# Query blocks taken together in the first block's attention

## The chip, the cores and the metric

One core of a Trainium2 chip runs one program. The metric is the device time of one execution in microseconds, the median of the timed runs. The core has five engines that each run their own instruction list in order and meet at semaphores: TensorE (PE, with weight loads shown as PEld), VectorE (DVE), ScalarE (ACT), GpSimd (POOL) and SyncE (SP), which issues most DMAs.

## The reference

Two blocks of two layers each on one sequence of 512 positions, width 1024. The change touches only the attention of the first block. Each of its layers has three kinds of attention:

```python
oa = diff_attention(...)              # 4 heads, each the difference of two softmax maps; bias, causal
ob = mla_attention(...)               # 8 heads; scores = nope part + rope part; causal
oc = sliding_window_attention(...)    # 8 heads; window of 128 keys, sinks, bias
y = (gates[:, :, 0] * ((oa * silu(a_z)) @ w_br_a[l])
     + gates[:, :, 1] * ((ob * silu(b_z)) @ w_br_b[l])
     + gates[:, :, 2] * ((oc * silu(c_z)) @ w_br_c[l]))
x = x + rms_norm(y @ w_out[l], norm_post[l])
x = x + sigmoid(x @ w_ple_gate[l]) * (p[l] @ w_ple_proj[l])
```

In all three the query block i of 128 positions sees key blocks up to i: i+1 blocks in the first two, at most two blocks in the third. Retention, a dilated attention and two gated feed-forwards make the second block.

## The kernel before

All projections multiply weights split into a high and a low float32r part with an activation split the same way: three matmuls of 128x128 by 128x512 for each k-tile (method `kt`, lines L714 to L716), eight k-tiles for most output tiles. Weights stream in chunks of eight k-tiles through a ring of three slots; ACT makes the high part (L1250), POOL the low (L565, L567).

The attention of a layer is twelve items, n = 0 to 11: four of kind da (differential), four mla, four sw (sliding window). An item is a pair of maps or heads, m = 0 and 1, one on rows 0 to 63 of the array and one on rows 64 to 127. Its queries come in four blocks i. The steps for one block are

- scores on PE (`scores`, L852, for mla also L858 for the rope part) into banks 3 and 4, one for each m;
- maxima on DVE (`maxima`, L1882, L1887 or L1885): the bias or mask is added and the row's maximum taken, the scores go to SBUF (`probs`, two buffers for each m, block i uses number i % 2);
- the exponential with its sum on ACT (`exps`, L1388);
- probabilities on DVE (`probs`, L1900, L1904 or L1906 and L1909): divided by the sum; in da the two maps are joined;
- transposes on PE (`turn`, L879) into bank 5, for mla and sw also bank 6;
- a copy to SBUF on ACT (`copies_out`, L1398);
- values on PE (`values`, L899) into bank 7.

Around and between these lie the projections that later steps need. `ORDER[n]` lists the projection tiles beside item n, `STEPS[n]` their k-tiles, and `cuts(n)` gives the nine places at which the list is broken off. In items 0 to 6 the places are even: PE fills up to the first, gives the scores of block 1, fills, turns block 0, fills, gives scores of block 2 and values of block 0, and so on. From item 7 on (`ONE_PLACE`) two neighbouring places are one. Every engine follows the same list by `cuts`: what DVE evicts (`beside`, L1973 and others) and ACT converts stands between the attention steps in the same order.

Projection tiles, and the small column sums (`sum_da`, `sum_q`, `sum_kv`, L768) and row spreads (`row_*`, L777) among them, open the banks 0 to 2 in turn (`rotate(3)`). PE waits on the semaphore `evicted` when it opens a bank whose last tile DVE has not taken. In item 2 the list begins bkv, sum_da, sum_q, v; in item 3 kr, sum_kv, sum_da, cv. DVE's output of the item before (`out`, L1913, L1920) lies between `maxima(n, 0)` and `probs(n, 0)`, and for da items waits for ACT's square (L1415).

```python
for n in range(12):
    at_ = cuts(n)
    for i in range(QT):
        fill(n, at_[2 * i])
        if i + 1 < QT:
            scores(n, i + 1)
        if i:
            values(n, i - 1)
        fill(n, at_[2 * i + 1])
        turn(n, i)
```

Of the kernel before, what the change touches and what calls it, by code (L numbers as in the profile page):

```python
# [20 lines left out]
ALU = mybir.AluOpType  # L21
ACT = mybir.ActivationFunctionType

P = 128
# [77 lines left out]

def cuts(n):
# [203 lines left out]
def two_stacks_kernel(nc, d, out):  # L307
# [3 lines left out]
    with ExitStack() as ctx:  # L311
# [343 lines left out]
        def _(pe):  # L655
            t = Tally(pe)

            class Programs:
# [121 lines left out]
                def mix(self, l):  # L780
# [58 lines left out]
                    def scores(n, i):  # L839
                        kind = KINDS[n]  # L840
                        kb, blocks = key_blocks(kind, i)
                        keys = CK if kind == "sw" else AK
                        if i == 0:
                            pe.wait_ge(sems["evicted"], self.scored_on + 1)
                        t.up("scored", 2)
                        if self.steps:
                            pe.wait_ge(sems["scored"], t.at("scored"))
                        self.steps += 1
                        q, kk = slice(i * P, (i + 1) * P), slice(kb * P, (kb + blocks) * P)
                        for m in range(2):  # L850
                            r = slice(64 * m, 64 * m + 64)
                            ins = pe.matmul(banks[S0 + m][:, 0:blocks * P], AQ[r, q], keys[r, kk], start=True, stop=(kind != "mla"))  # L852
                            if kind != "mla":
                                ins.then_inc(sems["s_ready"], t.one("s_ready"))
                        if kind == "mla":
# [13 lines left out]
                    def turn(n, i):  # L869
                        _, blocks = key_blocks(KINDS[n], i)  # L870
                        if t.k.get("pt_copied", 0):
                            pe.wait_ge(sems["pt_copied"], t.at("pt_copied", CREDITS["pt_copied"]))
                        if i == 0:
                            pe.wait_ge(sems["v_token"], t.at("v_token"))
                        for m in range(group(KINDS[n])):
                            t.up("probs")
                            pe.wait_ge(sems["probs"], t.at("probs"))
                            for b in range(blocks):
                                ins = pe.transpose(banks[TURN + m][:, b * P:(b + 1) * P], SS[i % 2][m][:, b * P:(b + 1) * P], ID[:])  # L879
# [3 lines left out]
                    def values(n, i):  # L883
                        kind = KINDS[n]
                        kb, blocks = key_blocks(kind, i)
                        if i == 0:
# [4 lines left out]
                        for b in range(blocks):  # L891
                            for m in range(group(kind)):
                                r = slice(64 * m, 64 * m + 64)
                                if kind == "da":
                                    r, p = slice(0, P), PT[i % 2]
                                    v = VT[:, kb + b, :]
                                else:
                                    v, p = (CV if kind == "sw" else VT)[:, kb + b, r], PT[m]
                                ins = pe.matmul(banks[OUTB][r, i * P:(i + 1) * P], v, p[:, b * P:(b + 1) * P],  # L899
                                                start=(b == 0), stop=(b == blocks - 1))  # L900
# [16 lines left out]
                    for n in range(12):  # L917
                        at_ = cuts(n)
# [8 lines left out]
                        fill(n, at_[8])  # L927
# [1630 lines left out]
```

## Time and profile before

| | |
|---|---|
| Median of 3 runs | 2990.86 us (2988.71 to 2991.18) |
| Profiled execution, its own time | 2991.07 us |
| Its span | 2989.2 us |
| PE, PEld busy | 2949.5 us (99%), 2360.9 us (79%) |
| DVE, ACT, POOL busy | 1740.0 us (58%), 1055.6 us (35%), 1280.3 us (43%) |
| Attention of the first block with its projections | about 35 to 560 us and 600 to 1130 us |

The span is from the first to the last instruction; the execution's own time is 1.9 us longer. Durations in a timeline are from start to end, and matmuls overlap, so the time that one takes from the stream is read from one start to the next. A matmul of float32 operands appears as two in the counts. Item numbers and layers are read off the order of the lines.

### The profile page before, as it was taken

The numbers are of one execution on the slowest core, as the hardware profiler recorded it, in microseconds if no ns is written. First come the engines' busy times: TensorE is split into PE (matmuls) and PEld (weight loads), VectorE is DVE, ScalarE is ACT, GpSimd is POOL, SyncE is SP. The second block draws the span as 40 slices with busy tenths as digits, with TensorE's granted clock in tenths as the row PEclk, the third lists the DMA queues.
The fourth block names the chain that finished last, engine by engine and source line by source line (L and its number), as shares of the span: only waits on it lengthen the run. The fifth ranks groups of instructions, "written<-read, shape, count | busy, mean of one in ns | idle before, by whom it ended". The sixth has DMA issues, their size and how long they took to land.

```text
span 2989.2 us, 39167 instructions
## 1 busy us (share of the span) xinstructions
PE 2949.5 (99%) x15272; PEld 2360.9 (79%) x15272; DVE 1740.0 (58%) x3028; ACT 1055.6 (35%) x1875; POOL 1280.3 (43%) x926
## 2 busy tenths in 40 slices
PE   8999999999999999999999999999999999999999
PEld 6777777887777778788888788887888888788887
DVE  4765455475745555646553587615766666587722
ACT  4443343354343432533333322224333333432222
POOL 3333334453333345444444455544434334355543
PEclk9999999999999999999999999999999999999999
DMA  5222223232222223232222233332222222223332
GB/s 194 81 78 65 71 78 98 85 110 73 78 64 71 77 86 96 87 99 85 85 82 84 82 99 99 95 95 90 84 78 71 78 78 78 71 85 99 99 94 76
DMA packets 78332, 260.22 MB, mean 87 GB/s; under 512 B 10731, under 2 KB 13547, under 8 KB 78149
## 3 DMA queue, kind: packets, MB, share of 16 engines
q1 hardware_dynamic: 77572, 255.63, 27.6%
q8 instruction: 122, 2.00, 0.3%
q10 hardware_dynamic: 576, 2.10, 0.2%
q14 instruction: 62, 0.50, 0.1%
HBM read 255.53 MB, written 6.09 MB: 88 GB/s over the span
## 4 chain that ended last, share of the span: by engine, by line
PE 93%; DVE 3%; ACT 1%; DMA 1%; issue 1%; POOL 0%; SPq 0%; DVEq 0%; ACTq 0%
PE bank L714 25%; PE bank L716 25%; PE bank L715 24%; PE bank L852 2%; PE bank L899 2%; PE bank L879 1%; PE bank L731 1%; PE bank L732 1%; PE bank L738 1%; PE bank L1016 1%; PE bank L1017 1%; PE bank L1022 1%; PE bank L1111 1%; PE bank L768 1%; DMA bias_copies<-bias_vectors 1%
## 5 line engine op out<-in xcount | busy, mean ns | idle before, releaser
L565 POOL TENSOR_TENSOR w_lo<-w_raw,w_hi 128x512 fp32r<-128x512 f32 x458 | 609.8, 1332 | 1627.5 <-ACT w_hi L1250 1627.5
L714 PE MATMUL bank<-h_hi,w_hi 128*128 128x512 f32 x2367 | 944.7, 399 | 0.8 <-POOL w_lo L565 0.8
L716 PE MATMUL bank<-h_hi,w_lo 128*128 128x512 f32 x2367 | 924.6, 391 | 0.0
L715 PE MATMUL bank<-h_lo,w_hi 128*128 128x512 f32 x2367 | 923.3, 390 | 0.0
L1250 ACT CAST w_hi<-w_raw 128x1024 fp32r<-128x1024 f32 x458 | 480.1, 1050 | 1234.9 <-PE bank L716 1138.1
L567 POOL TENSOR_TENSOR w_lo<-w_raw,w_hi 128x512 fp32r<-128x512 f32 x458 | 667.3, 1457 | 35.9
L714 PEld LDWEIGHTS bank<-h_hi,w_hi 128*128 128x128 f32 x2367 | 445.4, 188 | 97.9 <-issue 9.3
L716 PEld LDWEIGHTS bank<-h_hi,w_lo 128*128 128x128 f32 x2367 | 445.1, 188 | 96.0
L715 PEld LDWEIGHTS bank<-h_lo,w_hi 128*128 128x128 f32 x2367 | 445.9, 188 | 86.4 <-issue 0.3
L2128 DVE TENSOR_SCALAR m<-bank,gains 128x512 f32<-128x512 f32 x48 | 36.1, 751 | 328.6 <-ACT ta L1453 197.0
L1388 ACT ACTIVATE probs<-probs,small_columns 128x128 f32<-128x128 f32 (+2 forms) x192 | 101.9, 531 | 168.6 <-DVE small_columns L1887 164.4
L716 PE MATMUL bank<-f_hi,w_lo 128*128 128x512 f32 x352 | 136.9, 389 | 0.0
L714 PE MATMUL bank<-f_hi,w_hi 128*128 128x512 f32 x352 | 136.9, 389 | 0.0
L715 PE MATMUL bank<-f_lo,w_hi 128*128 128x512 f32 x352 | 136.9, 389 | 0.0
L1882 DVE CUSTOM_DVE_ANT_0 probs<-bank,bias 128x256 f32<-128x256 f32 (+3 forms) x128 | 56.4, 441 | 93.8 <-PE bank L852 90.1
L1398 ACT COPY pt<-bank 128x256 f32<-128x256 f32 (+3 forms) x160 | 55.5, 387 | 62.3 <-PE bank L879 62.2
L714 PE MATMUL bank<-zo_hi,w_hi 128*128 128x512 f32 x192 | 77.3, 403 | 0.0
L715 PEld LDWEIGHTS bank<-f_lo,w_hi 128*128 128x128 f32 x352 | 66.1, 188 | 13.8
L716 PEld LDWEIGHTS bank<-f_hi,w_lo 128*128 128x128 f32 x352 | 66.1, 188 | 13.8
L714 PEld LDWEIGHTS bank<-f_hi,w_hi 128*128 128x128 f32 x352 | 66.1, 188 | 13.5
L731 PE MATMUL bank<-h_hi,w_hi 128*128 128x512 f32 x161 | 68.3, 424 | 8.2 <-ACT h_hi L1316 4.9
L716 PE MATMUL bank<-zo_hi,w_lo 128*128 128x512 f32 x192 | 75.0, 391 | 0.0
(321 smaller groups left out, 4473.2 us busy)
## 6 DMA issues: line engine op xcount, KB each, us to landing
w_raw<-in_w SPq DMA_DIRECT2D x458, 512.0 KB, 3.5
bias_copies<-bias_vectors SPq DMA_DIRECT2D x1, 2560.0 KB
x_res<-in_x_t ACTq DMA_DIRECT2D x4, 512.0 KB, 8.1
bias<-bias_copies SPq DMA_DIRECT2D x8, 256.0 KB, 3.3
bias<-bias_copies SPq DMA_DIRECT2D x16, 128.0 KB, 2.4
out_x<-x_res SPq DMA_DIRECT2D x8, 256.0 KB, 2.5
bias_copies<-bias_vectors SPq DMA_DIRECT2D x1, 1280.0 KB
ple_raw<-in_p_t SPq DMA_DIRECT2D x2, 512.0 KB, 3.7
```

Of the source, the lines that this page charges most:

```text
L565: pool.tensor_tensor(WL[slot][:, 0:half], RAW[slot][:, 0:half], WH[slot][:, 0:half].bitcast(F32), ALU.subtract).then_inc(sems["lo_half"], 1)
L567: pool.tensor_tensor(WL[slot][:, half:], RAW[slot][:, half:], WH[slot][:, half:].bitcast(F32), ALU.subtract).then_inc(sems["lo_done"], 1)
L714: pe.matmul(banks[bank][:], WH[slot][:, w], hi[:, k, :], start=start, stop=False)
L715: pe.matmul(banks[bank][:], WH[slot][:, w], lo[:, k, :], start=False, stop=False)
L716: pe.matmul(banks[bank][:], WL[slot][:, w], hi[:, k, :], start=False, stop=stop).then_inc(sems["kt_done"], 1)
L731: pe.matmul(banks[bank][:], WH[slot][:, w], hi[:, k, :], start=start, stop=False)
L852: ins = pe.matmul(banks[S0 + m][:, 0:blocks * P], AQ[r, q], keys[r, kk], start=True, stop=(kind != "mla"))
L899: ins = pe.matmul(banks[OUTB][r, i * P:(i + 1) * P], v, p[:, b * P:(b + 1) * P], start=(b == 0), stop=(b == blocks - 1))
L1250: act.copy(WH[slot][:], RAW[slot][:]).then_inc(sems["hi_done"], t.one("hi_done"))
L1388: act.activation(s, s, ACT.Exp, bias=sm(NM + u), accum_out=sm(DEN + u)).then_inc(sems["exped"], t.one("exped"))
L1398: act.copy(p[:, 0:w], banks[TURN + m][:, 0:w]).then_inc(sems["pt_copied"], t.one("pt_copied"))
L1882: dve.tensor_tensor_reduce(SS[i % 2][m][:, 0:w], banks[S0 + m][:, 0:w], bias, 1.0, LOWEST, ALU.add, ALU.max, sm(MX + u)).then_inc(sems["dv ...
```

## The change

Query blocks whose scores fit one bank of 512 columns are taken together as one part: blocks 0 and 1 (128 + 256 columns) in da and mla, then 2 and 3 alone; blocks 0 and 1 and blocks 2 and 3 (256 + 256) in sw. The steps run once for each part. Inside a part the blocks lie side by side (`placed_blocks`), each with its own matmuls, maximum, exponential, reciprocal and scaling as before; the transposes of a part end in one semaphore step, and ACT copies the part's whole width at once. The buffers alternate by a count of parts over all items (`parity`). `cuts` makes 2 x parts + 1 places. The number of tiles and k-tiles and their order are the same.

```diff
+TOGETHER = {"da": ((0, 1), (2,), (3,)), "mla": ((0, 1), (2,), (3,)), "sw": ((0, 1), (2, 3))}
+def n_parts(n):
+    return len(TOGETHER[KINDS[n]])
+def parity(n, part):
+    return (sum(n_parts(x) for x in range(n)) + part) % 2
+def placed_blocks(kind, part):
+    at_, placed = 0, []
+    for i in TOGETHER[kind][part]:
+        w = key_blocks(kind, i)[1] * P
+        placed.append((i, at_, w))
+        at_ += w
+    assert at_ <= SEQ
+    return placed
 def cuts(n):
-    total = sum(k for _, k in ORDER[n])
+    total, parts = sum(k for _, k in ORDER[n]), n_parts(n)
     if n >= ONE_PLACE:
...
-        places = [upto(n, round(third / 3 * (p + 1))) for p in range(3)] + [upto(n, total - BEHIND)]
+        early = max(parts - 1, 2)
+        places = [upto(n, round(third / early * (p + 1))) for p in range(parts - 1)] + [upto(n, total - BEHIND)]
         return [x for place in places for x in (place, place)] + [len(STEPS[n])]
     first = PRE if n == 0 else 0
-    share = (total - first) / 9
-    return [upto(n, round(first + share * (p + 1))) for p in range(9)]
+    share = (total - first) / (2 * parts + 1)
+    return [upto(n, round(first + share * (p + 1))) for p in range(2 * parts + 1)]
...
-                    def scores(n, i):
+                    def scores(n, part):
...
+                        placed = placed_blocks(kind, part)
+                        t.up("scored", 2 * len(placed))
+                        for i, at_, w in placed:
+                            kb = key_blocks(kind, i)[0]
+                            q, kk = slice(i * P, (i + 1) * P), slice(kb * P, kb * P + w)
                             for m in range(2):
                                 r = slice(64 * m, 64 * m + 64)
-                                pe.matmul(banks[S0 + m][:, 0:blocks * P], AR[r, q], KR[r, kk], start=False, stop=True).then_inc(sems["s_ready"], t.one("s_ready"))
+                                ins = pe.matmul(banks[S0 + m][:, at_:at_ + w], AQ[r, q], keys[r, kk], start=True, stop=(kind != "mla"))
+                                if kind != "mla" and i == placed[-1][0]:
+                                    ins.then_inc(sems["s_ready"], t.one("s_ready"))
...
-                        for i in range(QT):
+                        for i in range(parts):
                             fill(n, at_[2 * i])
-                            if i + 1 < QT:
+                            if i + 1 < parts:
                                 scores(n, i + 1)
...
                         for m in range(2):
+                            for i, at_, w in placed_blocks(kind, part):
+                                u = 2 * i + m
...
+                                dve.tensor_tensor_reduce(SS[parity(n, part)][m][:, at_:at_ + w], banks[S0 + m][:, at_:at_ + w], bias, 1.0, LOWEST, ALU.add, ALU.max, sm(MX + u)).then_inc(sems["dve_step"], t.one("dve_step"))
```

On PE, in a sw item, this stood before where block 2's scores, block 0's values and block 1's transposes are given (probs_71 and probs_72 hold block 1's probabilities of m = 0 and 1):

```order
L716 MATMUL bank<-h_hi,w_lo 128x512
L852 MATMUL bank<-c_k,att_q 128x256 x2
L899 MATMUL bank<-pt_73,c_v 64x128
L899 MATMUL bank<-pt_74,c_v 64x128
L879 MATMUL bank<-ident,probs_71 128x128 x2
L879 MATMUL bank<-ident,probs_72 128x128 x2
L714 MATMUL bank<-h_hi,w_hi 128x512
```

and this stands in the same item now, where the scores of blocks 2 and 3 and the transposes of blocks 0 and 1 are given:

```order
L746 MATMUL bank<-h_hi,w_lo 128x512
L884 MATMUL bank<-c_k,att_q 128x256 x4
L912 MATMUL bank<-ident,probs_69 128x128 x3
L912 MATMUL bank<-ident,probs_70 128x128 x3
L744 MATMUL bank<-h_hi,w_hi 128x512
```

Two pairs of score matmuls now follow each other, and all transposes of two blocks; the sw item is broken off at three places in place of five, the last scores and values at its end counted.

On DVE, at the head of item 2 (the 128 and 256 columns are blocks 0 and 1; rstd in L1920 is the output of item 1, lat_q the tile bkv), before:

```order
L1887 TENSOR_SCALAR small_columns<-small_columns 128x1
L1913 SCALAR_TENSOR_TENSOR ta<-ta,tc 128x512
L1920 SCALAR_TENSOR_TENSOR rstd<-bank,ta 128x512
L1900 RECIPROCAL small_columns<-small_columns 128x1 x2
L1906 TENSOR_SCALAR probs_70<-probs_70,small_columns 128x128
L1909 SCALAR_TENSOR_TENSOR probs_69<-probs_69,small_columns,probs_70 128x128
L1882 ISA probs_71,small_columns<-bank,bias 128x256
```

and now:

```order
L1921 TENSOR_SCALAR small_columns<-small_columns 128x1
L1947 SCALAR_TENSOR_TENSOR ta<-ta,tc 128x512
L1954 SCALAR_TENSOR_TENSOR rstd<-bank,ta 128x512
L1934 RECIPROCAL small_columns<-small_columns 128x1 x3
L1940 TENSOR_SCALAR probs_70<-probs_70,small_columns 128x128
L1943 SCALAR_TENSOR_TENSOR probs_69<-probs_69,small_columns,probs_70 128x128
L1934 RECIPROCAL small_columns<-small_columns 128x1
L1940 TENSOR_SCALAR probs_70<-probs_70,small_columns 128x256
L1943 SCALAR_TENSOR_TENSOR probs_69<-probs_69,small_columns,probs_70 128x256
L1916 ISA probs_71,small_columns<-bank,bias 128x384
```

The eviction of bkv (lat_q) comes behind the next two maxima in both; ahead of it now stand two more maxima, one more pair of reciprocals, two more scalings, and maxima of 384 columns in place of 256. In item 3 the same stands ahead of kr.

## Rows read from the trace of the kernel before

**Rows 1.** The page, part 4: shares of the last chain by engine.
```profile
PE 93%; DVE 3%; ACT 1%; DMA 1%; issue 1%; POOL 0%; SPq 0%; DVEq 0%; ACTq 0%
```

**Rows 2.** Waits of PE: line, releaser, total us, times, longest us.
```profile
PE bank L777 <- DVE att_q L1987: 1.5, 2, 0.9
...
PE bank L879 <- DVE probs L1909: 0.9, 1, 0.9
```

**Rows 3.** Timeline of PE, item 8, layer 0: start, duration, line, operands.
```profile
346.44 0.39 PE L714 MATMUL bank<-h_hi,w_hi 128*128 128x512 f32 x1
...
347.12 0.39 PE L714 MATMUL bank<-h_hi,w_hi 128*128 128x512 f32 x1
...
347.89 0.70 PE L852 MATMUL bank<-c_k,att_q 64*128 64x256 f32 x4
348.53 0.44 PE L879 MATMUL bank<-ident,probs 128*128 128x128 f32 x2
348.72 0.48 PE L714 MATMUL bank<-h_hi,w_hi 128*128 128x512 f32 x1
...
349.50 0.40 PE L714 MATMUL bank<-h_hi,w_hi 128*128 128x512 f32 x1
```

**Rows 4.** Timeline of PE, mla items, layer 0: a long and a short part.
```profile
247.08 1.02 PE L858 MATMUL bank<-k_rope,att_qr 64*128 64x512 f32 x4
248.04 0.66 PE L899 MATMUL bank<-pt,att_vt 128*64 128x128 f32 x8
248.63 0.50 PE L714 MATMUL bank<-h_hi,w_hi 128*128 128x512 f32 x1
...
263.39 0.39 PE L858 MATMUL bank<-k_rope,att_qr 64*128 64x128 f32 x4
263.71 1.09 PE L899 MATMUL bank<-pt,att_vt 128*64 128x128 f32 x16
264.74 0.66 PE L865 MATMUL bank<-ident,var 128*128 128x128 f32 x4
```

**Rows 5.** Timeline of PE, item 2, layer 0: from its first scores.
```profile
107.81 0.49 PE L852 MATMUL bank<-att_k,att_q 64*128 64x128 f32 x4
...
109.58 0.47 PE L714 MATMUL bank<-h_hi,w_hi 128*128 128x512 f32 x1
...
116.00 0.95 PE L768 MATMUL bank<-ones,da_sq 128*128 128x1 f32 x8
116.81 1.93 PE L768 MATMUL bank<-ones,lat_sq 128*128 128x1 f32 x16
118.60 0.63 PE L714 MATMUL bank<-h_hi,w_hi 128*128 128x512 f32 x1
```

**Rows 6.** Timeline of DVE, item 2, layer 0.
```profile
108.52 0.28 DVE L1882 CUSTOM_DVE_ANT_0 probs<-bank,bias 128x128 f32<-128x128 f32 x1
...
109.58 1.35 DVE L1913 SCALAR_TENSOR_TENSOR ta<-ta,tc 128x512 f32<-128x512 f32 x1
111.38 0.69 DVE L1920 SCALAR_TENSOR_TENSOR rstd<-bank,ta 128x512 f32<-128x512 f32 x1 [0.45 <-ACT da_sq L1415]
...
113.41 0.43 DVE L1882 CUSTOM_DVE_ANT_0 probs<-bank,bias 128x256 f32<-128x256 f32 x1 [0.17 <-PE bank L852]
...
114.07 0.42 DVE L1882 CUSTOM_DVE_ANT_0 probs<-bank,bias 128x256 f32<-128x256 f32 x1
...
116.20 0.69 DVE L1973 TENSOR_TENSOR lat_q<-bank,rstd 128x512 f32<-128x512 f32 x1 [1.51 <-PE bank L716]
```

**Rows 7.** DVE groups by shape, 35 to 1100 us: count, busy us, mean ns.
```profile
L1909 DVE SCALAR_TENSOR_TENSOR probs<-probs,small_columns,probs 128x256 f32<-128x256 f32 x8 | 8.7, 1088 | 0.3
...
L1906 DVE TENSOR_SCALAR probs<-probs,small_columns 128x256 f32<-128x256 f32 x8 | 6.5, 815 | 0.3
...
L1906 DVE TENSOR_SCALAR probs<-probs,small_columns 128x384 f32<-128x384 f32 x8 | 3.8, 479 | 0.3
```

**Rows 8.** Windows: us, busy by engine (instructions), granted clock, DMA share, GB/s.
```profile
118.60:122.44 3.84, 3.84 (x12) 2.94 (x12) 1.88 (x6) 2.86 (x6) 1.32 (x2) 0.56 0.32 93
```

More of the change, by code:

```diff
@@ L848, in scores @@
                         self.steps += 1
[L849 to L854, printed above, removed]
@@ L867, in turn_values, with turn, values @@
                         t.up("v_token")
-                    def turn(n, i):
-                        _, blocks = key_blocks(KINDS[n], i)
+                    def turn(n, part):
                         if t.k.get("pt_copied", 0):
                             pe.wait_ge(sems["pt_copied"], t.at("pt_copied", CREDITS["pt_copied"]))
-                        if i == 0:
+                        if part == 0:
                             pe.wait_ge(sems["v_token"], t.at("v_token"))
                         for m in range(group(KINDS[n])):
-                            t.up("probs")
+                            t.up("probs", len(TOGETHER[KINDS[n]][part]))
                             pe.wait_ge(sems["probs"], t.at("probs"))
-                            for b in range(blocks):
-                                ins = pe.transpose(banks[TURN + m][:, b * P:(b + 1) * P], SS[i % 2][m][:, b * P:(b + 1) * P], ID[:])
+                            for b in range(part_width(KINDS[n], part) // P):
+                                ins = pe.transpose(banks[TURN + m][:, b * P:(b + 1) * P], SS[parity(n, part)][m][:, b * P:(b + 1) * P], ID[:])
                             ins.then_inc(sems["turned"], t.one("turned"))
                             t.up("pt_copied")
-                    def values(n, i):
+                    def values(n, part):
                         kind = KINDS[n]
-                        kb, blocks = key_blocks(kind, i)
-                        if i == 0:
+                        if part == 0:
                             t.up("o_used")
@@ L890, in values @@
                         pe.wait_ge(sems["pt_copied"], t.at("pt_copied", CREDITS["pt_copied"]))
[L891 to L900, printed above, removed]
+                        for i, at_, w in placed_blocks(kind, part):
+                            kb, blocks = key_blocks(kind, i)
+                            for b in range(blocks):
+                                for m in range(group(kind)):
+                                    r = slice(64 * m, 64 * m + 64)
+                                    if kind == "da":
+                                        r, p = slice(0, P), PT[parity(n, part)]
+                                        v = VT[:, kb + b, :]
+                                    else:
+                                        v, p = (CV if kind == "sw" else VT)[:, kb + b, r], PT[m]
+                                    ins = pe.matmul(banks[OUTB][r, i * P:(i + 1) * P], v, p[:, at_ + b * P:at_ + (b + 1) * P],
+                                                    start=(b == 0), stop=(b == blocks - 1))
                         ins.then_inc(sems["pv_done"], t.one("pv_done"))
@@ L1415, in mix @@
                             act.activation(SQA[:], banks[OUTB][:], ACT.Square).then_inc(sems["da_squared"], t.one("da_squared"))
[L1416 removed]
+                        for i in range(parts):
                             beside(n, at_[2 * i])
[L1418 removed]
+                            if i + 1 < parts:
                                 exps(n, i + 1)
@@ L1861, in mix, with maxima @@
                         dve.wait_ge(sems["gains_in"], 16)
-                    def maxima(n, i):
+                    def maxima(n, part):
                         kind = KINDS[n]
-                        w = key_blocks(kind, i)[1] * P
                         step = len(self.turns)
```

126 lines of the change are left out of this document (64 added, 62 removed).

## The prediction

> **What bounds the kernel.** I read the chain of waits by engine first: TensorE (PE) carries 93% of it, ScalarE (ACT) 1% [rows 1]. So the time is PE's own instruction stream, and only two things can move it: fewer microseconds that PE needs for the same matmuls, or waits of PE. Then I read PE's waits: in both attention stages together few are left; of those the change can touch there are 0.9 us before a transpose and 1.5 us before a spread of a row [rows 2]. Then PE's timeline around the places where attention work interrupts the projections, for what a switch costs. Last the timelines of PE and of VectorE (DVE) over item 2, because it is DVE that must free the banks in which PE accumulates.
>
> **What a switch costs now.** Between float32r matmuls the step of one k-tile (three matmuls) is 0.68 us (346.44 to 347.12). The step into scores is 0.77, so 0.09 goes into the entry; the first k-tile after an interruption takes 0.78 (348.72 to 349.50), so 0.10 goes into the exit [rows 3]. A pair of score matmuls with two key blocks lasts 0.64 until the transposes start [rows 3]. The mla pairs give the slope: 0.96 for four blocks, 0.32 for one, so 0.213 a block and 0.107 fixed for each pair [rows 4]. The 0.64 is then 0.43 of work, 0.107 of the pair and 0.107 more for leaving it. Values of mla and sw: 0.59 for two blocks, 1.03 for four, so 0.22 a block and 0.15 fixed [rows 4]. Transposes: 0.19 for two, which is their work alone [rows 3]. In da the values use all 128 rows and columns, and I give them no fixed cost.
>
> The Trainium skill ("TensorEngine Tiling (Array Packing)", Key Properties) says that changing the tiling mode drains the engine, while another tile of the same mode does not. By that rule, the trace agrees: the cost sits at the passage between full-array matmuls and the 64-row or 64-column ones. What the rule would add is the last rival below.
>
> **Part by part: matmuls.** Columns, transposes, exps and maxima are as many as before; every weight tile is used as before. What goes is switches.
> - sw item (8 of them in the two layers). Before, five interruptions: scores+turn; scores+values+turn, twice; values+turn; scores+values. Five times 0.19 for entry and exit, four score pairs at 0.21, four value groups at 0.15: 2.4 us. After, three: scores(2,3)+turn; values+turn; scores(0,1)+values. 3x0.19 + 2x0.21 + 2x0.107 for the second pair in a part + 2x0.15 = 1.5. Saved 0.89.
> - da item (8). The interruption that held only scores(1) goes: 0.19 + 0.21, less 0.107 for the second pair now behind scores(0): 0.29.
> - mla item (8). The same, but a pair has two halves (nope and rope): 0.19 + 0.21 - 0.21, and one value group less, 0.15: 0.34; I take 0.35.
> Sum: 8 x (0.89 + 0.29 + 0.35) = 12.2 us saved. No row shows a second pair of queries in one bank right behind the first. The nearest row is the mla passage from the nope to the rope pair, 0.107 [rows 4]. Bounds: if the second pair costs 0.213, as the standalone one does, 0.21 + 0.11 + 0.21 less are saved in an item of the three kinds, 7.9 in all; if it costs nothing, the same more, 16.5.
>
> **Activations and copies.** ACT makes 104 copies in place of 160 and the same exps. I cost this at nothing, since PE's work hides it (ACT's share of the chain is 1% [rows 1]). Where its queue counts is below.
>
> **Waits that go.** The 0.9 before the first item's transpose: the turn of item 0 now lies nine k-tiles behind its scores, not seven, 1.4 us more, against two more maxima and exps; gone: -0.9. The 1.5 before the spread of a row stands on a late eviction; the cuts move, and I take half: -0.7 (0 to -1.5).
>
> **Waits that come.** DVE runs its program in order. At the head of each item it now works on blocks 0 and 1 before it evicts the first tile of the item. In most items PE does not need that bank for two more tiles (over 10 us). Items 2 and 3 differ: two column sums take the two other banks of the three, so the tile v (cv) opens in the bank of bkv (kr), right behind the sums. Item 2, layer 0:
> - PE now: scores at 107.81, projections from 109.58, sums from 116.00, v opens at 118.60 [rows 5]. After: block 1's pair stands ahead of item 2's projections, +0.54 (0.43 of work, 0.11 fixed), and the scores that interrupt bkv are 384 wide in place of 256, +0.21: 118.60 + 0.54 + 0.21 = 119.35.
> - DVE now: maxima from 108.52, two blocks in 1.06; then the gate product at 109.58; then at 111.38 the output, 0.45 late behind ACT's square; the next maxima at 113.41; a 256-wide one steps 0.66; then it waits 1.51 for PE to finish bkv, and evicts at 116.20 [rows 6]. After: 2 x 0.66 more maxima; ACT's exps and then its square follow them, so the output too comes 1.3 later, at 112.7. From there 1.9 as now, plus block 1's probabilities, 0.36 for two reciprocals, 0.82 and 1.09 [rows 7]: 116.9. Two maxima of 384 columns (0.53 at 128, 0.66 at 256, so 0.79 each): 118.4, eviction 0.7: 119.1. PE asks at 119.35: on time, but the 0.82 and 1.09 are means over instructions that differ widely: 384 columns of the first line took 0.48 [rows 7]. With both that short DVE comes 0.95 earlier, and I allow as much later. Stall 0.2 (0 to 0.7).
> - Item 3 is the same with two sums of four matmuls, 1.6 (0.81 is one such group, 116.00 to 116.81) in place of 2.6 [rows 5]: PE asks 1.0 earlier: stall 0.8 (0 to 1.7).
> Both layers: +2.0 (0 to 4.8). Queued behind DVE's late eviction are its own later evictions, which have two tiles of slack.
>
> **The clock.** After item 2's sums the granted clock was 0.56 over 118.60 to 122.44 [rows 8], that is mostly at 1.2 instead of 2.4 GHz; it cost 0.44 x 3.84 = 1.7 us. It had stood at full before the sums, 2.6 us with hardly a moving column. In item 3 the sums were only 1.6 us, now 1.6 + 0.8 of stall = 2.4. I take half a drop for each layer: 2 x 0.5 x 1.7 = +1.7 (0 to 3.4).
>
> **Sum.** -12.2 - 0.9 - 0.7 + 2.0 + 1.7 = -10.1. The profiled execution took 2991.07 us around a span of 2989.2, within 0.2 us of the median 2990.86. 2991.07 - 10.1 = 2981.0.
>
> **Rivals.**
> - A, the second pair is a full pair: only 7.9 saved. -7.9 - 0.9 - 0.7 + 2.0 + 1.7 = -5.8, 2985.3. For it: no row shows such a pair. Against: the nope and rope pairs. 15%.
> - B, the bank is late and the clock falls: stalls at 4.8, both drops of item 3 in full: -12.2 - 0.9 + 4.8 + 3.4 = -4.9, 2986.2. For it: the spread of these two lines. 15%. The Trainium skill ("TensorE: Matmul & The Clock Gate", HAM oscillation) says that gaps between bursts of matmuls bring the half-rate clock back each time; by that rule, the trace agrees with the drop after item 2's sums.
> - C, nothing is saved: entry and exit cost the same microseconds wherever the work lies, so fewer switches give nothing; 2.0 + 1.7 - 1.6 = +2.1, 2993.2. Against: 0.09 and 0.10 are seen at each switch. 5%.
> - D, slower: the probabilities of blocks 0 and 1 come too late for their turn. At the head of the 14 items 0 to 6 of both layers DVE has 1.3 us of maxima and 2.3 of probabilities more (worked out above). If PE waits there 1.2 us in each (17) on top of B's stalls, 17 + 4.8 + 3.4 - 12.2 = +13, 3004. From 0.7 us an item on the result is slower by more than 6. For it: PE already waited once for probs, 0.9 [rows 2]. Against: 11.4 k-tiles, 7.8 us, lie between scores and turn in place of 8.9, 6.0 us. 7%.
> - E, a second pair costs nothing at all: -16.5 + 2.1 = -14.4, 2976.7. This is the result by the tiling page's rule, on which tiles of one mode need no drain. Against: the 0.107 of nope to rope, both of one mode. 5%.
> My forecast has 53%.
>
> **Numbers.** No change means within 0.2%, 6 us, about what a measurement of this kernel can tell. Faster by more, below 2984.9: nearly all of the forecast, E and some of A and B: 0.60. Within: the rest of A and B, C and part of the forecast's upper end: 0.33. Slower: 0.07. The range reaches from just below E to above B: 2976.5 to 2989.5.
>
> **What would show it.** In the changed profile: PE's score line with as many matmuls; new PE waits in the list, on the eviction of lat_q and of k_rope, 0 to 1.7 us each; the wait for probs in item 0 gone; in a sw item three interruptions in place of five; the granted clock after item 3's sums below 1. I am wrong if the sw items keep their length, or if PE waits for DVE at the start of many items.

## The result and the profile after

The changed kernel is faster, by more than twice what was forecast and outside the range: 2967.36 us (median of 4 runs, 2966.18 to 2968.73) against 2989.78 us (2987.26 to 2991.18), a ratio of 0.9928, interval 0.9914 to 0.9942. That is 22.4 us gained where 10 were forecast. The profiled execution took 2968.73 us around a span of 2966.9 us; before it was 2989.2.

The chain of waits, by engine, stands as in [rows 1]: PE sets the end.

```profile
PE 93%; DVE 4%; ACT 2%; issue 1%; DMA 0%; POOL 0%; SPq 0%; DVEq 0%; ACTq 0%
```

PE's waits in the attention of layer 0, 35 to 560 us (line, releaser, total, times, longest), to be read beside [rows 2]. The spread's wait on att_q is gone in both layers. In item 0 the wait for probs is 0.6 instead of 0.9, but a longer one stands ahead of it, on the maxima of blocks 0 and 1 (1.3; before it was 0.4). This second wait differs from one execution of a kernel to the next: profiled again, the kernel before has 2.0 there, and the changed kernel 0.4 and 0.9. No projection line (L744) is in the list: PE never waits for an eviction in items 2 and 3.

```profile
PE bank L884 <- DVE small_columns L1921: 1.3, 1, 1.3
PE bank L884 <- DVE att_k L2007: 0.8, 1, 0.8
PE bank L912 <- DVE probs L1943: 0.6, 1, 0.6
```

PE's timeline in the same place of item 8 as [rows 3] (start, duration, line, operands). Scores of blocks 2 and 3 now follow each other.

```profile
344.76 0.39 PE L744 MATMUL bank<-h_hi,w_hi 128*128 128x512 f32 x1
...
345.53 1.14 PE L884 MATMUL bank<-c_k,att_q 64*128 64x256 f32 x8
346.59 0.88 PE L912 MATMUL bank<-ident,probs 128*128 128x128 f32 x6
347.22 0.47 PE L744 MATMUL bank<-h_hi,w_hi 128*128 128x512 f32 x1
...
348.00 0.40 PE L744 MATMUL bank<-h_hi,w_hi 128*128 128x512 f32 x1
```

Into the scores the step is again 0.77. The two pairs last 1.06 (345.53 to 346.59) where one lasted 0.64: the second costs 0.42, which is what the prediction gave to its columns (0.43), and nothing more. The fixed 0.107 that it gave to each pair isn't paid again.

The same in mla, where the blocks 0 and 1 of the next item are given at the end of item 4, beside [rows 4]. The first pair of block 1 (257.93) takes 0.44, which is two blocks at 0.213 and 0.01 more. The four pairs take 1.51 until the values; by the prediction's prices they would take 4 x 0.107 + 6 x 0.213 = 1.71.

```profile
257.38 0.49 PE L884 MATMUL bank<-att_k,att_q 64*128 64x128 f32 x4
257.71 0.39 PE L890 MATMUL bank<-k_rope,att_qr 64*128 64x128 f32 x4
257.93 0.60 PE L884 MATMUL bank<-att_k,att_q 64*128 64x256 f32 x4
258.37 0.60 PE L890 MATMUL bank<-k_rope,att_qr 64*128 64x256 f32 x4
258.89 1.09 PE L933 MATMUL bank<-pt,att_vt 128*64 128x128 f32 x16
```

Item 2, layer 0. PE's timeline, beside [rows 5]: v opens at 118.03, straight behind the sums.

```profile
106.60 0.93 PE L884 MATMUL bank<-att_k,att_q 64*128 64x128 f32 x8
...
115.44 0.95 PE L798 MATMUL bank<-ones,da_sq 128*128 128x1 f32 x8
116.25 1.93 PE L798 MATMUL bank<-ones,lat_sq 128*128 128x1 f32 x16
118.03 0.48 PE L744 MATMUL bank<-h_hi,w_hi 128*128 128x512 f32 x1
```

DVE's timeline, beside [rows 6]. The added probabilities (256 columns) take 0.41 and 0.48, and lat_q is evicted from 116.18 to 116.86: 1.17 us before PE asks. The prediction's sum had it 0.25 early, and allowed a stall of 0.2.

```profile
107.73 0.29 DVE L1916 CUSTOM_DVE_ANT_0 probs<-bank,bias 128x128 f32<-128x128 f32 x1 [0.34 <-PE bank L884]
...
111.71 0.69 DVE L1954 SCALAR_TENSOR_TENSOR rstd<-bank,ta 128x512 f32<-128x512 f32 x1 [0.62 <-ACT da_sq L1449]
...
113.87 0.41 DVE L1940 TENSOR_SCALAR probs<-probs,small_columns 128x256 f32<-128x256 f32 x1
114.32 0.48 DVE L1943 SCALAR_TENSOR_TENSOR probs<-probs,small_columns,probs 128x256 f32<-128x256 f32 x1
...
116.18 0.68 DVE L2007 TENSOR_TENSOR lat_q<-bank,rstd 128x512 f32<-128x512 f32 x1
```

The groups of DVE by shape, beside [rows 7] (count | busy, mean ns | idle before): all eight of 256 columns are short now, at 0.48 and 0.41 in place of 1.09 and 0.82. Those of 384 columns have a longer mean than before.

```profile
L1943 DVE SCALAR_TENSOR_TENSOR probs<-probs,small_columns,probs 128x384 f32<-128x384 f32 x8 | 8.6, 1073 | 0.3
L1940 DVE TENSOR_SCALAR probs<-probs,small_columns 128x384 f32<-128x384 f32 x8 | 6.7, 843 | 0.3
...
L1943 DVE SCALAR_TENSOR_TENSOR probs<-probs,small_columns,probs 128x256 f32<-128x256 f32 x8 | 3.9, 484 | 0.3
L1940 DVE TENSOR_SCALAR probs<-probs,small_columns 128x256 f32<-128x256 f32 x8 | 3.3, 412 | 0.3
```

Item 3 was close. On PE the last sums begin at 154.44 and cv opens at 155.33; DVE evicts kr from 154.53 to 155.21. The margin is 0.12 us.

```profile
154.44 1.03 PE L798 MATMUL bank<-ones,da_sq 128*128 128x1 f32 x8
155.33 0.47 PE L744 MATMUL bank<-h_hi,w_hi 128*128 128x512 f32 x1
```

```profile
154.53 0.68 DVE L2012 TENSOR_TENSOR k_rope<-bank,rstd 128x512 f32<-128x512 f32 x1
```

The window behind item 2's sums, beside [rows 8]: the granted clock (third from the end) is 1.00, where it was 0.56.

```profile
117.90:122.00 4.10, 4.10 (x22) 3.42 (x22) 2.88 (x6) 3.39 (x7) 2.60 (x2) 1.00 0.12 19
```

**Where the time went.** The starts of the k-tiles, matched one by one between the traces, give each item's change in length (layer 0, layer 1, us; an item runs from its first k-tile to that of the next, so block 1's scores of the next item count in it):

| Item | 0 | 1 | 2 | 3 | 4 | 5, 6 each | 7 | 8, 9, 10 each | 11 |
|---|---|---|---|---|---|---|---|---|---|
| Layer 0 | +0.67 | -0.50 | -2.07 | -0.75 | -0.54 | -0.69 | -0.94 | -1.05 | -1.48 |
| Layer 1 | -0.02 | -0.51 | -0.47 | -0.97 | -0.54 | -0.69 | -0.94 | -1.05 | -1.48 |

They sum to -19.6. A further -4.4 lies outside these items (-0.95 of it before the first k-tile of item 0), and +1.7 behind the last k-tile: -22.3, the difference of the spans. Item 0 of layer 0 is what differs most between executions of one kernel, by its waits.

### The profile page after: what moved, and what is told of

Its sections match the earlier page's. It is cut to its first block, busy times and chain, and to the rows that moved or that the text cites. A ratio compares the mean times of both kernels' runs of the same rounds, so it can differ in the third digit from the quotient of the medians.

```text
span 2966.9 us, 39047 instructions
## 1 busy us (share of the span) xinstructions
PE 2928.3 (99%) x15272; PEld 2361.9 (80%) x15272; DVE 1717.2 (58%) x3028; ACT 1050.7 (35%) x1819; POOL 1275.4 (43%) x926
## 4 chain that ended last, share of the span: by engine, by line
PE 93%; DVE 4%; ACT 2%; issue 1%; DMA 0%; POOL 0%; SPq 0%; DVEq 0%; ACTq 0%
PE bank L744 25%; PE bank L746 25%; PE bank L745 25%; PE bank L884 2%; PE bank L933 2%; PE bank L912 1%; PE bank L761 1%; PE bank L762 1%; PE bank L768 1%; PE bank L1050 1%; PE bank L1051 1%; PE bank L1056 1%; PE bank L798 1%; PE bank L1145 1%; PE bank L1088 1%
## 5 line engine op out<-in xcount | busy, mean ns | idle before, releaser
L744 PE MATMUL bank<-h_hi,w_hi 128*128 128x512 f32 x2367 | 939.9, 397 | 0.2 <-POOL w_lo L595 0.2
L744 PEld LDWEIGHTS bank<-h_hi,w_hi 128*128 128x128 f32 x2367 | 444.8, 188 | 98.6 <-issue 10.8
L744 PE MATMUL bank<-f_hi,w_hi 128*128 128x512 f32 x352 | 136.9, 389 | 0.0
L744 PEld LDWEIGHTS bank<-f_hi,w_hi 128*128 128x128 f32 x352 | 66.1, 188 | 13.8
L744 PE MATMUL bank<-zo_hi,w_hi 128*128 128x512 f32 x192 | 76.2, 397 | 0.0
L2029 DVE SCALAR_TENSOR_TENSOR tb<-gate_t,bank 128x512 f32<-128x512 f32 x32 | 22.0, 687 | 92.3 <-ACT gate_t L1400 51.9
L745 PE MATMUL bank<-zo_lo,w_hi 128*128 128x512 f32 x192 | 74.8, 390 | 0.0
```

The lines of the kernel that those rows point to most:

```text
L744: pe.matmul(banks[bank][:], WH[slot][:, w], hi[:, k, :], start=start, stop=False)
L745: pe.matmul(banks[bank][:], WH[slot][:, w], lo[:, k, :], start=False, stop=False)
```

## The experiments

Theory F, formed on this comparison: what costs is the passage between shapes and the break of the k-tile run, while a second pair behind a first costs its columns only; and DVE has the margins that the trace shows (1.17 and 0.12 us). The rivals are named with each run. The letters change their meaning on the way: in the first two expectations S is this theory and F the forecast's sizes; from the split pair on F is this theory and S the forecast's. The kernel before was run beside all of them.

**The parts alone, and both kernels again.** The grouping in sw only, in da and mla only, and the kernel before and the changed kernel profiled once more.

```diff
-TOGETHER = {"da": ((0, 1), (2,), (3,)), "mla": ((0, 1), (2,), (3,)), "sw": ((0, 1), (2, 3))}
+# the sw part alone
+TOGETHER = {"da": ((0,), (1,), (2,), (3,)), "mla": ((0,), (1,), (2,), (3,)), "sw": ((0, 1), (2, 3))}
+# the da and mla part alone
+TOGETHER = {"da": ((0, 1), (2,), (3,)), "mla": ((0, 1), (2,), (3,)), "sw": ((0,), (1,), (2,), (3,))}
```

> Parts of two blocks in the sw items alone; da and mla keep four parts. Theory S (a second score pair behind the first has no fixed cost, 0.107 us less than forecast; no new wait): the four sw items of a layer together 4.2 us shorter than before in PE's timeline, 8.5 us in both layers, time about 2981.5 +- 2. Rival F (the sizes of the forecast are right, 0.107 for a second pair, and the rest of the gain came through waits or the clock): 0.89 an item, 7.1 us, and an item at 33.3 us in place of 33.1. Rival G (the missing gain is made of clock drops that went away): the items as in F, and whatever is more than 7 us stands in stretches at half clock.

> Parts of two blocks in da and mla items alone; sw keeps four parts. Theory S: what sw_only leaves of the attention's gain, 0.5 us for a da item and 0.69 for an mla item, 9.5 less the waits of the first item, about 8.5 us, time about 2981.5 +- 2; both kernels' gains add up to the whole change's, clock apart. Rival F: 0.29 and 0.35 an item, 5.1 us, time about 2985. No wait of PE on the evictions of lat_q or k_rope in any of the theories now, since DVE evicted k_rope 0.1 us before PE asked in the changed kernel.

> The kernel before, profiled once more, for the stretches at half clock. If their length after the first linear stage of each layer and at item 2 belongs to the kernel, they are as in the first profile: 3.4 us at item 2 of both layers and 6.8 us at the end of both linear stages. If it is chance of one execution, one or more of them are absent or of the other length.

> The changed kernel, profiled once more. If the clock's part of the gain belongs to the kernel: no stretch at half clock at item 2 of layer 0, one at item 2 of layer 1, 3.4 us at the end of both linear stages, as in its first profile. If it is chance, they differ from that, and the PE timeline between them does not.

Measured: sw alone 2978.77 us (6 runs; ratio 0.9970, interval 0.9958 to 0.9982); da and mla alone 2978.57 (5 runs; 0.9966, 0.9953 to 0.9978); the kernel before, 10 runs beside them, 2989.35. So the parts gave 10.6 and 10.8 us, 21.4 together. The whole gave 22.4, and 21.3 when it was timed again (below): they add up. By the k-tiles, sw alone takes 4.2 us out of each layer, 8.4 in both: +0.44 in item 7, whose end now holds block 1's scores of item 8, -1.05 in each of items 8 to 10, and -1.48 in item 11. Da and mla alone take 10.2 out of items 1 to 7 of both layers and item 0 of layer 1, of which 1.5 is the wait on att_q (it is absent from this kernel's trace and stands in that of sw alone), so 8.7 in switches. Together 17.1. The prediction had 7.1 for sw and 5.1 for da and mla. So the expectations' S holds, with 4.2 for the sw items of a layer; the forecast's sizes fall, and so does rival G, since the missing gain stands in every sw item and not in stretches of low clock. The trace has no wait on lat_q or k_rope, as expected. Its item 0 of layer 0, left out of this sum, is 2.5 longer than in the kernel before: PE waits 2.4 for the maxima there, and the granted clock is 0.57 from 48 to 52 us. This is one execution; the medians' 10.8 show no such loss.

The two repeats show what one execution can tell: the kernel before had a span of 2985.3 us instead of 2989.2, the changed kernel 2968.4 instead of 2966.9. The items agree to 0.01 to 0.03 us, except for item 0's waits and where a stretch of low clock came or stayed away. In the changed kernel's repeat it came behind item 2's sums of layer 0, and cost 1.6 us there; in the repeat of the kernel before it stayed away behind those of layer 1, which made that item 1.55 us shorter. So these stretches come and go with the execution, the second case of both expectations. Of the places behind item 2's sums the clock falls in three of four in the two traces of the kernel before, and in five of six in the three of the changed kernel.

**An entry and an exit more.** The values of the item before are put between the scores of block 0 and of block 1 of the next item, in 22 places.

```diff
                         if n + 1 < 12:
-                            scores(n + 1, 0)
-                        values(n, parts - 1)
+                            scores(n + 1, 0, lambda: values(n, parts - 1))  # called between its two blocks
+                        else:
+                            values(n, parts - 1)
```

> Nothing is added here but the order on TensorE: at the end of each of items 0 to 10 of both layers (22 places) the values matmuls of the item before are put between the scores of block 0 and those of block 1 of the next item, where the changed kernel has both blocks' scores in one piece. In the changed kernel's trace two blocks' scores in one piece take 0.43 us longer than one block's, which is their matmuls alone; the 64-row pairs are left once. Theory F (a change of shape is what costs, and a second pair behind the first costs its work only): one more entry and one more exit in each place, 0.09 to 0.10 us and 0.10 to 0.11 us, so +4.2 to +5 us over the changed kernel (about 2971.5 to 2972.5 us). Theory L (only leaving the 64-row pairs costs, going into them is free): 22 x 0.107 = +2.4 us, about 2970. Theory S (the forecast's: each pair has its fixed 0.107 us wherever it stands): the same pairs are issued, so +0, about 2967.5. The tenth of the time that is uncertain between executions is 1 to 2 us, so the trace decides by the starts of the k-tiles: from the last k-tile of an item to the first of the next, 0.19 to 0.22 us more by F, 0.11 by L, 0 by S.

Measured: 2977.41 us (5 runs; ratio to before 0.9967, interval 0.9955 to 0.9979), 10 above the changed kernel: twice what F gave, and far from L and S. PE's timeline at the end of item 8:

```profile
368.54 0.49 PE L886 MATMUL bank<-c_k,att_q 64*128 64x128 f32 x4
368.96 1.09 PE L935 MATMUL bank<-pt,c_v 128*64 128x128 f32 x16
369.98 0.70 PE L886 MATMUL bank<-c_k,att_q 64*128 64x256 f32 x4
370.61 0.50 PE L744 MATMUL bank<-h_hi,w_hi 128*128 128x512 f32 x1
```

The same matmuls (24 in the counts) take 2.07 us here and 1.88 in one piece in the changed kernel:

```profile
365.63 0.93 PE L884 MATMUL bank<-c_k,att_q 64*128 64x128 f32 x8
...
367.51 0.50 PE L744 MATMUL bank<-h_hi,w_hi 128*128 128x512 f32 x1
```

By the k-tiles an item gets longer by 0.16 to 0.20 where the values are those of mla or sw and by 0.32 to 0.36 in items 0 to 2, where they are those of da, which use the whole array; for both layers 14 x 0.17 + 8 x 0.35 = 5.2. So S (a pair costs the same wherever it stands) falls, and L (0.11 each) too; F's size of 0.19 to 0.22 lies between the two kinds. The other 5 us were in no theory. For 2.8 of them the trace has a cause: block 1's maxima come later, and with them kr's eviction, whose margin was 0.12 us. PE now waits 0.55 and 0.56 there, and in layer 1 a stretch of low clock follows at once (0.60 from 777 to 781 us; 1.7 us), while in layer 0 the clock stays full. A further 2.5 lies outside the items, where two traces of the changed kernel differ by 1.2; its cause is not shown.

```profile
157.19 0.50 PE L744 MATMUL bank<-h_hi,w_hi 128*128 128x512 f32 x1 [0.55 <-DVE k_rope L2015]
```

**DVE late by a known sum.** Four, and in a second kernel two, memsets of a scratch tile in items 2 and 3.

```diff
                             if i + 1 < parts:
                                 maxima(n, i + 1)
+                            if n in (2, 3) and i == 0:
+                                for _ in range(4):      # range(2) in the second kernel
+                                    dve.memset(TB[:], 0.0).then_inc(sems["dve_step"], t.one("dve_step"))
+                                    dve.wait_ge(sems["dve_step"], t.at("dve_step"))
```

> VectorE gets four memsets of a scratch tile (about 1.9 us together) in items 2 and 3 of both layers, between the maxima of block 2's part and the side work, so everything behind them on VectorE comes 1.9 us later; the output is unchanged. In the changed kernel's trace TensorE opens the next product 1.85 us after the start of lat_q's eviction in item 2 (116.18 and 118.03) and 0.12 us after the end of k_rope's eviction in item 3 (155.21 and 155.33). Theory M (the margin read from the changed kernel's trace is the true one: the forecast's stall of 2.0 us for items 2 and 3 did not come because VectorE was in time by 1.17 us in item 2 and by 0.12 us in item 3): TensorE now waits some 0.7 to 0.8 us in item 2 and 1.7 to 1.8 us in item 3 of each layer, +4.5 to +5.2 us, about 2972 us, and the waits stand in the table of TensorE's waits at those products. Theory N (VectorE had other slack that the trace doesn't show, such as its own idle time behind the probabilities): the waits are shorter than 0.3 us and the time is within 1 us of the changed kernel, about 2967.5. If the clock falls behind the new waits, a further 1.7 us for each time.

> Two memsets in place of four in items 2 and 3. With four, VectorE's evictions came 2.63 us later (0.66 us each with their wait) and TensorE waited 1.4 us (item 2) and 2.4 us (item 3), as the margins of 1.17 and 0.12 us read from the changed kernel's trace give, and the granted clock fell behind the waits. Theory M now: 1.31 us late, so 0.1 us of wait in item 2, 1.2 us in item 3 of each layer, +2.6 us of waits. What is open is the clock: whether a wait of 1.2 us is followed by a low clock as those of 2.4 us were; if so 1.7 us more for each, about 2973.5 us in all, else about 2970.

Measured: 2982.50 us with four (10 runs; ratio 0.9980, interval 0.9970 to 0.9989), 2970.31 with two (1 run). The memsets step by 0.66 us, not 0.48, as each waits for the one before: DVE is 2.63 us late. With the margins 1.17 and 0.12 that makes waits of 1.46 and 2.51. PE's timeline, four memsets:

```profile
119.75 0.50 PE L744 MATMUL bank<-h_hi,w_hi 128*128 128x512 f32 x1 [1.38 <-DVE lat_q L2007]
...
161.27 0.68 PE L744 MATMUL bank<-h_hi,w_hi 128*128 128x512 f32 x1 [2.44 <-DVE k_rope L2012]
```

With two, 1.31 us late, item 3 waits 1.13 in layer 0 and 0.95 in layer 1 (1.2 by M):

```profile
157.14 0.50 PE L744 MATMUL bank<-h_hi,w_hi 128*128 128x512 f32 x1 [1.13 <-DVE k_rope L2012]
...
770.95 0.51 PE L744 MATMUL bank<-h_hi,w_hi 128*128 128x512 f32 x1 [0.95 <-DVE k_rope L2012]
```

So M holds, within 0.25 us: DVE has no slack but the margin, and every microsecond behind it is a microsecond of PE. With four the four waits are 7.5 us, yet the last k-tile comes 14.2 us later (15.1 by the medians). The rest is the clock: items 2 and 3 of the two layers are longer than their waits by 1.8, 1.7, 1.2 and 1.8 us, and behind each wait the granted clock is 0.50 to 0.60. Window behind item 3's wait in layer 0, four memsets:

```profile
161.00:165.00 4.00, 3.73 (x9) 2.92 (x10) 3.42 (x9) 0.30 (x2) 1.27 (x1) 0.57 0.42 121
```

and two memsets, layer 0 and layer 1:

```profile
158.00:162.00 4.00, 4.00 (x14) 3.12 (x13) 2.74 (x8) 0.92 (x4) 1.81 (x2) 0.57 0.29 73
771.00:775.00 4.00, 4.00 (x19) 3.30 (x20) 3.56 (x8) 1.73 (x4) 2.63 (x2) 1.00 0.13 16
```

After 1.6 us of sums and a wait of 2.4 or 2.3 us the clock is low in both layers; after the sums and 1.13 us it is low in layer 0, and after 0.95 us full in layer 1. With two memsets the clock also stays full behind item 2's sums in both layers, where the changed kernel's trace has one drop. So the one time of 2970.31, near the 2970 expected without a drop, holds one drop more and one less. The stall and the drop of rival B are real mechanisms of this place; in the changed kernel 0.12 us stood between PE and the stall.

**Fewer breaks.** The turn of a part at the same place as the next part's scores, in items 0 to 6 and then in items 1 to 6; the changed kernel once more beside the second.

```diff
     first = PRE if n == 0 else 0
+    if n:        # the first kernel has this for item 0 too, with (total - first) and first + share * (p + 1)
+        share = total / (parts + 1)
+        places = [upto(n, round(share * (p + 1))) for p in range(parts)]
+        return [x for place in places for x in (place, place)] + [len(STEPS[n])]
     share = (total - first) / (2 * parts + 1)
     return [upto(n, round(first + share * (p + 1))) for p in range(2 * parts + 1)]
```

> The changed kernel, with the turning of the probabilities put at the same place as the next part's scores in items 0 to 6 too, as items 7 to 11 have it: 3 interruptions fewer of the run of k-tiles in each of 7 items and 2 layers, 42 in all. Theory F (each interruption costs TensorE a fixed sum of its own, 0.03 us at least on the two k-tiles behind it, beside what its instructions take and what a change of shape costs): -1.3 us at 0.03 us each, up to -2.5 us at 0.06, so about 2965 to 2966, and the probabilities are still in time since the places lie further apart. Rival P (the probabilities of a part are now needed and asked for in the same place as its scores' successor, and VectorE and ScalarE have them later than that in the items with much side work, 2 and 3): TensorE waits for the turn at those places, 0.3 us or more in each of items 2 and 3, and the time is 2967.5 or above.

> The turning of the probabilities at the same place as the next part's scores in items 1 to 6 alone; item 0 keeps the changed kernel's places. In the kernel with this in items 0 to 6 each item from the second on was 0.15 to 0.25 us shorter (2.3 us in all over both layers), and item 0 of the first layer lost it again in a wait of 3.46 us on the probabilities, with the granted clock low behind it. Theory F (each interruption has a price of its own, some 0.06 us): those 2.3 us are now kept, about 2965.1 us, and TensorE's longest wait on probs is again 0.6 us. Rival P (the later probabilities cost something in the other items too, which the granted clock hid): no gain, 2967 us or above.

> The changed kernel once more, timed in more rounds beside the kernel above, for a narrower interval. The single parts alone measured 2978.77 and 2978.57 against 2989.35 us, so if they add up without meeting each other the changed kernel is at 2968.0, 21.4 us below the kernel before; if they meet (a wait that only both together take away), further below, as the first timing's 22.4 us would allow.

Measured: 2967.06 us for the first (5 runs; ratio 0.9933, interval 0.9920 to 0.9945), nothing gained over 2967.36. Items 1 to 6 each became 0.15 to 0.25 shorter (but for item 2 of layer 0, where the clock fell in this trace and had not in the changed kernel's). Item 0 of layer 0, though, has a wait for probs, and the window behind it a low clock:

```profile
52.18 0.85 PE L913 MATMUL bank<-ident,probs 128*128 128x128 f32 x3 [3.46 <-DVE probs L1944]
```

```profile
52.00:56.00 4.00, 3.82 (x12) 3.17 (x13) 3.16 (x12) 1.78 (x5) 2.49 (x2) 0.57 0.22 42
```

Rival P came true, in item 0, not in items 2 and 3. With item 0 left alone: 2965.81 us (4 runs, 2964.78 to 2965.91; ratio to before 0.9919, interval 0.9906 to 0.9933), beside 2967.49 us (5 runs, 2964.89 to 2967.65; 0.9921, 0.9908 to 0.9935) for the changed kernel. The trace has 2.2 us as F gave them, three breaks fewer in an item for 0.15 to 0.25 us, so 0.05 to 0.08 each; the times do not tell the two kernels apart, since the intervals overlap almost wholly. It is the fastest kernel of this study, by a gain that only the k-tiles show. The changed kernel's 2967.49 fits the 2968.0 of parts that do not meet.

## Why the prediction was wrong

The bottleneck, the places and the sign were right. What failed is the cost of a second score pair first, then two sizes. Each term as forecast, and as the first profiled executions have it:

| Term | Forecast | Measured |
|---|---|---|
| Switches | -12.2 | -17.2 |
| Waits of item 0 | -0.9 | +0.7 (1.97 now, 1.27 before) |
| Wait on att_q | -0.7 | -1.5 |
| Stalls on evictions, items 2 and 3 | +2.0 | 0 |
| Clock after item 3's sums | +1.7 | 0 |
| Low clock behind item 2, layer 0 | none | -1.6 |
| Outside the attention, and the tail | none | -4.4, +1.7 |
| Sum | -10.1 | -22.3 |

The -17.2 is -19.6 of the table of items without the three rows that are told apart (+0.7, -1.5, -1.6). The +0.7 is chance: profiled twice, the kernel before waits 1.3 and 3.0 in item 0, and the changed kernel, three times, 2.0, 0.7 and 1.4. The wait for probs, on which the forecast's -0.9 rested, went from 0.9 to between 0.2 and 0.6; the wait on the maxima ahead of it was in no term.

**The step that failed first: "0.107 fixed for each pair", carried over to the second pair in a bank.** It was taken from the passage of nope to rope in mla. The bound for a free second pair, 16.5, was within 0.7 us of the measured 17.2. Item by item: sw 0.89 + 2 x 0.107 = 1.10, measured 1.05; da 0.29 + 0.11 = 0.40 and mla 0.35 + 0.21 = 0.56, 7.7 for eight of each, measured 8.7. In the da and mla items one us is left over. The runs with fewer breaks show that a break in the k-tile run has a price of 0.05 to 0.08 of its own. In items 0 to 6 the places went from nine to seven, and the prediction priced only the one that held block 1's scores; the other held transposes alone. Fourteen such breaks at 0.05 to 0.08 are 0.7 to 1.1 us, an estimate that would account for it, but no run separates it. Rival E, given 5%, was the mechanism, though its time, 2976.7, missed too, since it kept the stalls and the drop of the clock. The Trainium skill ("TensorEngine Tiling (Array Packing)", Key Properties) says that another tile of the same mode needs no drain; the 1.06 against 0.64 us in item 8 agrees. The evidence weighed against it, the 0.107 of nope to rope, belongs to the first pair after a change of shape and to the last before one, not to each pair. The four pairs of the new mla trace show it: the first (257.38) takes 0.33, 0.12 more than its columns; the two in the middle take 0.22 (257.71, one block) and 0.44 (257.93, two blocks), 0.01 more; the last (258.37) takes 0.52, 0.09 more. [Rows 4] could not tell these two readings apart: both its pairs are the last before the values, and in the kernel before every pair was a first or a last one. That left the value open between the bounds, and did not carry the middle one with 53%.

**Second: the stalls.** The prediction added 0.82 and 1.09 us for the new probabilities of 256 columns, the means of [rows 7], though it named the spread. Single instructions of that shape before, in items 0 and 1:

```profile
51.69 0.41 DVE L1906 TENSOR_SCALAR probs<-probs,small_columns 128x256 f32<-128x256 f32 x1
...
81.01 1.37 DVE L1906 TENSOR_SCALAR probs<-probs,small_columns 128x256 f32<-128x256 f32 x1
```

The eight of that line took 0.41, 0.41, 0.57, 0.57, 0.91, 0.92, 1.36 and 1.37; the six longer ones all began while POOL was subtracting (from 80.94 to 82.23 beside the one shown). In the changed kernel none did, and all took 0.41 and 0.48. DVE began the eviction at 116.18 where 118.4 was worked out, PE asked at 118.03 where 119.35 was. PE's 1.32 is that item 2's scores begin 1.21 earlier (106.60, before 107.81) and that block 1's pair costs 0.43 and not 0.54. DVE's maxima begin 0.79 earlier (107.73, before 108.52), and of its other 1.4 the probabilities are 1.02. With DVE made late by known sums the stall came in full, so the mechanism stands and its size was off. That item 3 stayed clear by 0.12 us is luck: the split pair, which only reorders PE's matmuls, brought the stall.

**Third: the clock.** The drop after item 3 was tied to the stall and stayed away with it. The one after item 2's sums, read as a fact of the kernel from one execution, comes and goes with the execution: the same window of the changed kernel timed again has 0.57.

```profile
118.00:122.00 4.00, 4.00 (x14) 3.08 (x14) 2.85 (x6) 2.23 (x5) 2.56 (x2) 0.57 0.05 9
```

The -1.6 and most of the -4.4 are of this kind; the repeat of the kernel before, with no change at all, was 3.9 us shorter in its span, for the most part in the same places outside the attention. So of the 22.4 us some 18.7 are the change's own by the k-tiles (-17.2 - 1.5), and about 0.8 more if item 0's waits are averaged over all five traces. The timed runs agree: at a mean granted clock of 0.994 the kernel before took 2987.8 us (10 runs) and the changed kernel 2967.7 (6 runs), at 0.995 2984.9 (5 runs) and 2965.3 (3 runs), so at equal clock they are about 20 us apart. The remaining 2 or so go with the clock, whose mean was 0.9942 over 10 runs of the changed kernel and 0.9934 over 35 of the kernel before. Whether the change itself brings the slightly higher clock stays open.

**Right:** the wait on att_q went, the sw items have three breaks and are 1.05 shorter (0.89 forecast), the added work on DVE and ACT made PE wait nowhere outside item 0, and nothing came of rivals A, C and D. Why att_q is in time was not looked into; the grouping in da and mla does it. A and C fall with the second pair's 0.43 and the items' length; D with the absence of any wait for probs outside item 0.

## What to carry to other kernels

A fixed cost that is fitted to groups that each begin and end with a change of shape belongs to the change, until a row with two groups in a row says otherwise: price the second from 0 to the whole and put the value by what the mechanism would be. Before a mean goes into a race between two engines, look at its single instructions: a mean over 0.41 to 1.37 us, the long ones each beside another engine's work, makes a sum that need not occur. And a gain on the engine that sets the end shows itself to a hundredth of a microsecond in matched k-tiles, where medians that differ by 2 us cannot.

## What the runs showed of the hardware that was not expected

A scaling on DVE takes one duration when POOL is idle, and a longer one when POOL's subtraction is running as it begins: it then ends 0.1 to 0.55 us behind POOL. In the changed kernel a scaling of 384 columns begins together with POOL's subtraction and lasts 1.50 us; timelines of POOL, then DVE:

```profile
156.37 1.30 POOL L595 TENSOR_TENSOR w_lo<-w_raw,w_hi 128x512 fp32r<-128x512 f32 x1 [7.65 <-ACT w_hi L1284]
157.75 1.29 POOL L597 TENSOR_TENSOR w_lo<-w_raw,w_hi 128x512 fp32r<-128x512 f32 x1
```

```profile
156.38 1.50 DVE L1940 TENSOR_SCALAR probs<-probs,small_columns 128x384 f32<-128x384 f32 x1
157.92 1.53 DVE L1943 SCALAR_TENSOR_TENSOR probs<-probs,small_columns,probs 128x384 f32<-128x384 f32 x1
```

In the kernel with four memsets the same instruction comes after POOL has ended (POOL's last begins at 161.07 and takes 1.27) and lasts 0.48:

```profile
163.34 0.48 DVE L1940 TENSOR_SCALAR probs<-probs,small_columns 128x384 f32<-128x384 f32 x1
163.85 0.62 DVE L1943 SCALAR_TENSOR_TENSOR probs<-probs,small_columns,probs 128x384 f32<-128x384 f32 x1
```

Where DVE begins first it is DVE that keeps its short time, 0.75 for 512 columns, and POOL's subtraction that takes 1.77 us in place of about 1.3 (changed kernel, DVE, then POOL):

```profile
59.58 0.75 DVE L1943 SCALAR_TENSOR_TENSOR probs<-probs,small_columns,probs 128x512 f32<-128x512 f32 x1
```

```profile
59.71 1.77 POOL L595 TENSOR_TENSOR w_lo<-w_raw,w_hi 128x512 fp32r<-128x512 f32 x1 [2.28 <-ACT w_hi L1284]
```

In the attention stages of the kernel before, the changed one and the one with four memsets every long scaling begins while POOL is subtracting, or in two cases 0.03 us ahead of it, and no short one does; it was not tried by itself. The Trainium skill ("SBUF — State Buffer", SBUF: two separate sides) calls the ports that VectorE and GpSimd share an exclusive lock, which the one that starts first holds for its whole instruction. By that rule, the trace agrees on who waits. The wait isn't simply added: the two scalings above end 0.21 and 0.41 us behind POOL's end, where alone they take 0.48 and 0.62.

The other is how dear a wait of PE can be: 7.5 us of waits became 14.2 us of time, the rest by stretches with a granted clock of 0.50 to 0.60 behind them.
